# Four rows of one token block of an output projection placed ahead of the wait for the last attention head, in a two-layer hybrid decoder

## The reference

```python
def sb_dilated_mixer(h, w_in, rel_bias, w_out):
    ...
    oc = stick_breaking(hc(qc), hc(kc), hc(vc)).reshape(bsz, s_len, SB_W)
    ...
    od = dilated_mixture(hd(qd), hd(kd), hd(vd), rel_bias).reshape(bsz, s_len, DIL_HEADS_PER_GROUP * DIL_DH)
    y = jnp.concatenate([oc, od], axis=-1) @ w_out
    return y.astype(h.dtype)
...
            y = sb_dilated_mixer(hm, cd_w_in[j], rel_bias, cd_w_out[j])
        x = layer_norm(RES_ALPHA * x + (1.0 + g_m) * y, ln_g[layer, 0], ln_b[layer, 0])
        hf = x * (1.0 + sc_f) + sh_f
        yf = swiglu(hf, ffn_w1[layer], ffn_w3[layer], ffn_w2[layer])
```

## Time and profile before

| | |
|---|---|
| median of 3 runs | 1462.35 us (1462.13 to 1466.45) |
| profiled execution, its own time | 1465.9 us |
| its span | 1464.1 us |
| TensorE matmuls busy | 1370.0 us (94%), 6574 |
| VectorE busy | 635.4 us (43%), 821 |
| ScalarE busy | 449.3 us (31%), 603 |
| GpSimd busy | 513.1 us (35%), 209 |

### The profile page before, as it was taken

The page is one execution under the profiler, slowest core; times in us unless marked ns, Lnnn a source line. Parts: engine busy times, 40 slices in busy tenths (PEclk is TensorE's granted clock), DMA queues, the critical chain, the costliest instruction groups (busy, mean ns, idle before and its releaser), DMA issues.

```text
span 1464.1 us, 17183 instructions
## 1 busy us (share of the span) xinstructions
PE 1370.0 (94%) x6574; PEld 1131.9 (77%) x6574; DVE 635.4 (43%) x821; ACT 449.3 (31%) x603; POOL 513.1 (35%) x209
## 2 busy tenths in 40 slices
PE   4999998798999999999889999998889999999995
PEld 3878786587888888888778777788678888887884
DVE  4569761858644434400783333447485011010007
ACT  1343233424232232211332433325233232232221
POOL 2335332023454343544235212210225444444440
PEclk9899998899999999999999999998999999999998
DMA  9493542052456455752315421111113332234312
GB/s 331 144 75 127 188 144 86 16 187 72 146 199 223 151 199 176 250 113 93 120 61 200 115 77 58 58 44 43 58 58 101 100 100 86 100 84 146 100 58 58
DMA packets 93457, 173.81 MB, mean 119 GB/s; under 512 B 15655, under 2 KB 61879, under 8 KB 93276
## 3 DMA queue, kind: packets, MB, share of 16 engines
q1 hardware_dynamic: 90264, 169.63, 36.9%
q10 hardware_dynamic: 3140, 3.43, 0.9%
HBM read 170.87 MB, written 4.52 MB: 120 GB/s over the span
## 4 chain that ended last, share of the span: by engine, by line
PE 80%; DVE 10%; issue 7%; ACT 1%; POOL 1%; DMA 0%; DVEq 0%; POOLq 0%; ACTq 0%
PE ps L1019 14%; PE ps L1020 14%; PE ps L1021 14%; PE ps L1051 7%; PE ps L1053 7%; PE ps L1052 7%; PE ps L1145 2%; PE ps L1146 2%; PE ps L1147 2%; POOL w_lo L671 1%; PE ps L1442 1%; PE ps L1468 1%; PE ps L1456 1%; PE ps L1453 1%; PE ps L1158 1%
## 5 line engine op out<-in xcount | busy, mean ns | idle before, releaser
L671 POOL TENSOR_TENSOR w_lo<-raw,w_hi 128x1024 fp32r<-128x1024 f32 x205 | 512.9, 2506 | 915.8 <-ACT w_hi L691 915.7
L1019 PE MATMUL ps<-h_lo,w_hi 128*128 128x512 f32 (+2 forms) x1064 | 403.4, 379 | 13.1 <-DVE tmp L1886 6.2
L1020 PE MATMUL ps<-h_hi,w_hi 128*128 128x512 f32 (+2 forms) x1064 | 398.8, 375 | 0.0
L1021 PE MATMUL ps<-h_hi,w_lo 128*128 128x512 f32 (+2 forms) x1064 | 398.5, 374 | 0.0
L691 ACT ACTIVATE w_hi<-raw 128x1024 fp32r<-128x1024 f32 x205 | 216.1, 1056 | 473.6 <-PE ps L1053 185.9
L1019 PEld LDWEIGHTS ps<-h_lo,w_hi 128*128 128x128 f32 (+1 forms) x1064 | 204.8, 192 | 53.1 <-DVE tmp L1886 7.5
L1021 PEld LDWEIGHTS ps<-h_hi,w_lo 128*128 128x128 f32 (+1 forms) x1064 | 204.6, 192 | 35.3
L1020 PEld LDWEIGHTS ps<-h_hi,w_hi 128*128 128x128 f32 (+1 forms) x1064 | 205.2, 193 | 34.0
L1970 DVE TENSOR_TENSOR tmp<-tmp,ps 128x512 f32<-128x512 f32 x44 | 30.1, 688 | 265.2 <-PE ps L1021 265.2
L1051 PE MATMUL ps<-w_hi,hid_lo 128*128 128x512 f32 x352 | 137.2, 390 | 1.8 <-issue 0.9
L1052 PE MATMUL ps<-w_hi,hid_hi 128*128 128x512 f32 x352 | 137.0, 389 | 0.0
(11 more groups left out here) (233 smaller groups left out, 1519.8 us busy)
## 6 DMA issues: line engine op xcount, KB each, us to landing
raw<-wstream SPq DMA_DIRECT2D x205, 512.0 KB, 4.0
ada_raw<-astream SPq DMA_DIRECT2D x80, 512.0 KB, 4.1
ada_first<-astream SPq DMA_DIRECT2D x12, 512.0 KB, 9.7
ln_rows<-row_scratch SPq DMA_DIRECT2D x3, 1024.0 KB, 6.5
skew_scratch<-f_scratch ACTq DMA_DIRECT2D x1, 2304.0 KB
ada_first<-astream SPq DMA_DIRECT2D x8, 256.0 KB, 6.0
xa<-xT SPq DMA_DIRECT2D x4, 512.0 KB, 9.4
out<-xa SPq DMA_DIRECT2D x4, 512.0 KB, 3.5
```

Source lines behind the costliest of these rows:

```text
L671: nc.gpsimd.tensor_tensor(w_lo[:, slot, :], raw[:, slot % RAW, :], w_hi[:, slot, :].bitcast(F32), ALU.subtract).then_inc(sem("w_lo_ready"), 1)
L1019: pe.matmul(o, w_h, x_l, start=start, stop=False)
L1020: pe.matmul(o, w_h, x_h, start=False, stop=False)
L1021: return pe.matmul(o, w_l, x_h, start=False, stop=stop)
```

## The change

In `out_rows` for i = 2 alone, TensorE first does rows 0 to 3 of token block 2 (banks 4 and 5), each behind its slot and its input chunk. Only then come the wait for the last dilated head and the waits for the other banks. Rows 0 and 1 follow for blocks 0, 1 and 3; in the pass by blocks, block 2 has rows 4 and 5 left. The number of matmuls is the same.

```diff
@@ def out_rows(i, name, nk, x_h, x_l, ready, first_wait=None) @@
             first = SLOTS[name][0]
-            for s, v in out_free[i]:
-                pe.wait_ge(sem(s), v)
...
+            if i == 2:
+                for k in range(4):
+                    slot_waits(first + k)
+                    pe.wait_ge(sem(ready[0]), ready[1] + k + 1)
+                    rows_of(2, k)
+                pe.wait_ge(sem("h_tmp_ready"), H_BASE["cat1"] + 6)
+            for s, v in out_free[i]:
+                pe.wait_ge(sem(s), v)
+
             for k in range(nk - 4):
                 slot_waits(first + k)
                 pe.wait_ge(sem(ready[0]), ready[1] + k + 1)
-                for tb in (0, 1, 3, 2):
+                for tb in (0, 1, 3) if i == 2 else (0, 1, 3, 2):
...
             for tb in range(TB):
-                for k in range(nk - 4, nk):
+                for k in range(4 if i == 2 and tb == 2 else nk - 4, nk):
@@ after the last product with V @@
         pe.wait_ge(sem("nm_ready"), 1)
-        pe.wait_ge(sem("h_tmp_ready"), H_BASE["cat1"] + 6)
         out_rows(2, "out1", 6, h_hi, h_lo, ("h_ready", H_BASE["cat1"]))
```

## The result

| | before | changed |
|---|---|---|
| median of 20 runs each | 1465.24 us | 1470.18 us |
| lowest to highest | 1462.13 to 1469.57 | 1465.56 to 1475.51 |
| profiled execution, span | 1465.9, 1464.1 us | 1468.6, 1466.8 us |

The ratio of the changed kernel to the one before is 1.0031, with a 95% interval of 1.0023 to 1.0039. On 1465.24 us that is 4.5 us more (3.4 to 5.7). The three runs of before that the forecast started from (median 1462.35) lay at the low end: with 20 the median is 2.9 higher.

What follows compares the result with a forecast made beforehand. The prediction took the chain through TensorE (80%) as the bound, with a 4.2 us gap waiting for VectorE's last head. Residual 2, 3.4 us later, gave 1462.35 + 3.4 = 1465.8 us, range 1462.0 to 1469.5.

Steps and rivals of the forecast that it cites:

- What the moved work needs: Weight slots of block 2's rows: 0 and 1 ready, row 2 only at 1040.51 us, row 3 at 1042.91.
- Block 0 ready, VectorE: Projection to residuals: block 0 ready 4.0 us later, residual 2 queued behind residual 1 and 3.4 us later.
- TensorE's turn of blocks 0 and 1: TensorE's wait ahead of the turn grows from 0.59 to 3.5 us, at no further cost to the first FFN matmul.
- The sum: Whole program: +3.4 us on the median of 1462.35 gives 1465.8 us, 0.23% more.
- The unknown: the clock at the restart: TensorE's restart behind the new pause: low clock expected, twelve matmuls in 4.76 us; bounds +2.4 to +4.5 us in all.
- a clock that stays up: Rival at TensorE's restart: the clock does not fall in the pause, +2.4 us, 1464.8 us; chance 0.10.
- It works as meant: Rival: rows 2 and 3 ready, 24 matmuls run from 1032.31, residual 2 4.1 us earlier, 1458.3 us; chance 0.06.
- Clearly slower: Rival: low clock behind the wait for row 2 lasts beyond 1046.7; up to +4.5 us, 1466.9 us; chance 0.28.

Runs made afterwards that it cites:

- after_early: The changed kernel with ScalarE's high weight halves of rows 2 and 3 made ahead of the split of chunk 5; ratio to the kernel before 0.9964.
- the fills: Idle matmuls in TensorE's gap: 16 in the kernel before, ratio 0.9974; 22 in the changed kernel between rows 1 and 2 of block 2, ratio 1.0015.
- order_only: The changed kernel with block 2's rows 0 to 3 still first, but behind the wait for the last head; ratio to the kernel before 1.0021.
- two_rows: The changed kernel with only rows 0 and 1 of block 2 ahead of the wait; ratio to the kernel before 0.9959.
- order_fill: order_only with 16 idle matmuls in its gap, ahead of the wait for the last head; ratio to the kernel before 1.0009.

## Why the prediction was right and wrong

The mechanism held, the number did not: 1470.18 us lies 0.7 above the range.

- *What the moved work needs.* Right, and shown: rows 0 and 1 were issued in 2.6 us, then TensorE waited for row 2's slot and restarted at the place forecast, 1039.83 + 0.72 = 1040.55 for 1040.56. after_early took the late slots away and the cost with them.
- *Block 0 ready, VectorE.* Residual 0 was forecast 4.0 later than before and came 3.8 later; residual 2 3.4 later and came 3.0 later. The twelve matmuls of the restart, taken at 4.76 us, took 4.48 (from 1039.83 to 1043.38 and four more at 0.23), as the clock rose 3.6 us after the restart and not 4.2.
- *TensorE's turn of blocks 0 and 1.* The forecast let the second pause cost nothing. It was there (3.23 us for 3.5) and brought a second low clock, which cost 0.44 us through the slot that block 3's row 2 gives back. I had asked when block 3 would end at the low clock, and not when it gives that slot back. This made up for the 0.4 us too much of the step before, so the first FFN matmul came 3.47 later for 3.4, by two errors that cancel.
- *The sum, "on the median: 1462.35 + 3.4".* This is the step that failed. Its base, three runs, was 2.9 below what 20 give. The cost was 4.5 (3.4 to 5.7) for 3.4, and with 20 runs it can be told from no change. On a base of 1465.24 the forecast would have been 1468.6. The range did not cover the base either: one of the three runs lay 4.1 above their median, and I added 2.6. The profiled execution, forecast at 1469.3, took 1468.6, 0.72 of that by its head start.
- *The unknown: the clock at the restart.* I bounded the changed kernel's restart and held that of before fixed at the one trace. But the restart of before is as uncertain, and the fills show that it hangs more on the clock (1.94 us in the trace) than the changed kernel's (0.54). With neither low, the cost is 4.4 us, not the +2.4 that I gave for a clock that stays up: that bound compared a changed kernel at the full clock with a kernel before at the low one. The three restarts shown also differ in another way than I had it. The clock was low for 6.8 us from fall to rise in each (1033.9 to 1040.7 before, 1036.6 to 1043.4 changed, 1038.0 to 1044.8 in order_only). What moved is the fall, 1.6, 2.2 and 3.2 us behind the last matmul ahead of the pause, and so how much of the 6.8 us lay in the pause.
- *The rivals.* "It works as meant" needed the slots, and with them it came to -4.4 us at the first FFN matmul (4.1 worked out). "Clearly slower" was given 0.28 for a longer low clock at the restart; the time came out just over 0.3%, but its mechanism is not what the trace shows: the clock rose sooner than before.
- *Open.* Why 20 runs cost 4.5 us and the traces 3.5 is not settled; the interval reaches down to the trace. It goes with the clock. Each run's mean granted clock is on record (for before, of the 79 runs beside the experiments): 0.9614 on average in the changed kernel and 0.9622 in before, against 0.963 in both traces. Within a kernel the runs at a lower clock are the slower ones, 0.9 us for each 0.001 in changed and 0.9 to 1.5 us in before, so the 0.0008 between the two would make 0.7 to 1.2 us, an estimate. Which stretches are low more often in the changed kernel, the one trace of it does not show; the turn of blocks 2 and 3, where 1.6 us come and go, is a candidate.

## What to carry to other kernels

Before work is moved ahead of a wait, list everything that it needs and find for each the instruction that makes it and what that stands behind: here two of four weight slots were made behind the very wait that the work was to pass. An in-order queue then turns the early work into a roadblock, since what could have run at the old place stands behind it. Move no more than what is ready, keep the order in which the next engine wants the results, and fill such a gap with rows of all blocks instead of all rows of one.

## What the runs showed of the hardware

- A restart of TensorE behind a pause of about 4 us cost 1.9 us in the kernel before, almost half of the pause again. 16 matmuls without a use took it away, and the kernel became 0.26% faster (part of it, in the trace, at a later low clock). This is larger than I had expected of work that computes nothing. In two_rows a pause of 1.41 us left the clock up. Behind a pause of 3.2 us the granted clock fell in two traces and stayed at 1.00 in three, with the same instructions around it.
- The clock came back 3.6, 4.2 and 5.8 us after such restarts, with the same matmuls, 8, 9 and 13 of them slow. The Trainium skill ("TensorE: Matmul & The Clock Gate", Part 1) says that the number of slow matmuls varies between runs of one kernel. These are one trace each of three kernels, so they agree with it as far as they go.
- GpSimd's `w_lo` (4.73 us for two) beside VectorE's reciprocal of 64 x 512 from PSUM left that at 3.36 us. Beside the same GpSimd work VectorE's subtraction for `h_lo` (128 x 256) takes 2.43 us (1076.03 in the changed kernel); in order_fill it takes 2.41 us at 1074.73 and 0.41 at 1080.01, once GpSimd's two have ended at 1079.35. I had not expected the first to go free.
